# Forget sums and the split of the QKV weights moved into the QKV block; small loads of the modulation moved to ScalarE

## The reference, cut to what matters

```python
mod = (jax.nn.silu(c) @ w_ada + b_ada)[:, None, :]       # (1024) @ (1024, 6144)
sh1, sc1, g1, sh2, sc2, g2 = jnp.split(mod, 6, axis=-1)
h = rmsnorm(x, norm1_w) * (1 + sc1) + sh1
proj = h @ w_in                                          # z, x, B, C, dt | q, k, v | f
logf = jax.nn.log_sigmoid(f_raw + f_bias)                # per token and head, 8 heads
F_all = jnp.cumsum(jnp.concatenate([logf_prev, logf], axis=1), axis=1)
o = fox_attention(q, k_all, v_all, F_all[:, p0:], F_all, ...)   # scores + F_q - F_k
```

## Time and profile before

| what | us |
|---|---|
| median of 3 runs (lowest, highest) | 2694.07 (2690.8, 2696.57) |
| the profiled execution, its own time | 2693.54 |
| its span, first to last instruction | 2691.9 |
| busy: TensorE, VectorE, ScalarE, POOL | 2296.3, 1419.4, 944.6, 727.1 |
| mean granted clock of TensorE, of full | 0.921 |

### The profile page before, as it was taken

One profiled execution on the slowest core, in us unless ns is written; L12 is line 12 of the kernel. 1 busy time (PEld: TensorE's weight loads), 2 busy tenths in 40 slices (PEclk: granted clock), 3 DMA queues, 4 the chain that ended last, 5 costly groups with the idle time before them and its releaser, 6 DMA issues. The chain is left out here.

```text
span 2691.9 us, 35221 instructions
## 1 busy us (share of the span) xinstructions
PE 2296.3 (85%) x11464; PEld 1780.5 (66%) x11465; DVE 1419.4 (53%) x2897; ACT 944.6 (35%) x1628; POOL 727.1 (27%) x756
## 2 busy tenths in 40 slices
PE   3788989829999969999998599929999999999860
PEld 1687878726777845655564487718888888888650
DVE  1488878771001036666663567762445662435556
ACT  1354444321111114555554443321223441223533
POOL 0000101020000036777776002121323332222220
PEclk8899999959999969999999799959999999999985
DMA  6421211137774274544440644344657875557757
GB/s 194 162 73 64 78 59 70 48 119 249 256 260 171 104 170 113 111 92 86 86 85 18 226 150 143 120 165 109 186 173 242 270 246 153 161 157 220 226 188 265
DMA packets 190305, 408.39 MB, mean 152 GB/s; under 512 B 65274, under 2 KB 72728, under 8 KB 186784
## 3 DMA queue, kind: packets, MB, share of 16 engines
q1 hardware_dynamic: 161152, 304.51, 35.4%
q0 software_dynamic: 26672, 93.99, 12.8%
q10 hardware_dynamic: 2384, 8.65, 0.8%
HBM read 296.57 MB, written 110.53 MB: 151 GB/s over the span
## 5 line engine op out<-in xcount | busy, mean ns | idle before, releaser
L1391 POOL TENSOR_TENSOR c_acc<-c_acc,c_pr 128x512 f32<-128x512 f32 (+3 forms) x320 | 340.0, 1062 | 76.8 <-ACT c_pr L1513 34.8
L1513 ACT ACTIVATE c_pr<-c_ps,neg_f 128x512 f32<-128x512 f32 (+2 forms) x360 | 207.9, 595 | 162.7 <-PE c_ps L1457 154.4
L1543 DVE TENSOR_REDUCE c_mx<-c_pm 128x1 f32<-128x512 f32 (+3 forms) x304 | 178.8, 613 | 58.3 <-PE c_pm L1413 40.7
L1413 PE MATMUL c_pm<-c_km,c_q 66*128 66x512 f32 (+1 forms) x336 | 144.8, 447 | 22.6 <-DMA c_km<-f_k 16.5
L1176 DVE SCALAR_TENSOR_TENSOR b_lo<-b_pu,b_hi 128x512 fp32r<-128x512 f32 (+1 forms) x40 | 24.5, 612 | 258.7 <-ACT b_hi L1145 258.7
L258 PE MATMUL p_zx<-wa_hi,ah_hi 128*128 128x432 f32 x408 | 155.4, 381 | 3.6 <-DVE ah_lo L640 3.6
L258 PE MATMUL x_pg<-x_g_hi,x_x_hi 128*128 128x512 f32 x336 | 136.5, 406 | 24.8 <-DVE x_x_lo L2477 24.8
L607 POOL TENSOR_TENSOR yskip<-xs,params 128x512 f32<-128x512 f32 x17 | 21.6, 1268 | 497.6 <-ACT xs L545 497.6
L1466 PE MATMUL c_po<-c_pr,c_vv 128*64 128x512 f32 (+3 forms) x720 | 151.4, 522 | 0.0
L259 PE MATMUL p_zx<-wa_lo,ah_hi 128*128 128x432 f32 x408 | 150.2, 368 | 0.0
L260 PE MATMUL p_zx<-wa_hi,ah_lo 128*128 128x432 f32 x408 | 148.9, 365 | 0.0
(11 more groups left out here) (395 smaller groups left out, 5640.0 us busy)
## 6 DMA issues: line engine op xcount, KB each, us to landing
x_raw_g<-in_w_gate_dram SPq DMA_DIRECT2D x32, 1024.0 KB, 8.0
x_raw_u<-in_w_up_dram SPq DMA_DIRECT2D x32, 1024.0 KB, 8.6
x_raw_d<-in_w_down_dram SPq DMA_DIRECT2D x32, 1024.0 KB, 7.9
b_wa<-in_w_ada_dram POOLq DMA_DIRECT2D x16, 1024.0 KB, 7.6
c_k<-k_hi SPq DMA_DIRECT2D x14, 672.0 KB, 13.7
h_hi<-ah_hi SPq DMA_DIRECT2D x17, 512.0 KB, 2.6
h_lo<-ah_lo SPq DMA_DIRECT2D x17, 512.0 KB, 3.5
d_mix<-mix SPq DMA_DIRECT2D x17, 512.0 KB
```

The lines of the kernel that those rows point to most:

```text
L1391: pool.tensor_tensor(acc[:, ci % 2, cols], acc[:, ci % 2, cols], pr[:, i % RING, cols], ALU.add).then_inc(acc_done, 1)
L1413: last = pe.matmul(p_m[x % 2][:, 0:w * P], q2[0:KR, s, u["tile"] * P:(u["tile"] + 1) * P], km[:, s, kc], start=True, stop=not masked)
L1513: act.activation(pr[:, n % RING, cols], p_s[n % NPS][:, cols], ACT.Exp, bias=c.neg_f[:, it["h"], it["key"]:it["key"] + 1]).then_inc(exp_do ...
L1543: dve.tensor_reduce(mx[:, u % 2, pc["slot"]:pc["slot"] + 1], src, AX.X, ALU.max).then_inc(mx_done, 1)
```

## The change

In `modulation` the 11 small loads are issued by ScalarE at the head of its list. SP issues three slices of w_ada at once, into three places with a semaphore for each slice, and the fourth after the first chunk's products. `load_split_weights` has three places, so the load of slice k waits for the split of slice k - 3.

The stage `forget_sums` is gone. In the QKV block SP first issues two pairs of h, the last weight slice, the cached logs, and the third pair; ScalarE rounds the eight slices, VectorE splits all eight, and unit 0's products wait for each slice's split in turn. The sums become acts: after unit 0 the cached logs are transposed and the prompt's sum is taken, after units 1 and 2 the sum over the cached and the new tokens, after unit 3 the transposes of the 21 tiles. The negated halves of a sum lie in the memory of `b_wa`; each sum waits for the store of the one before, POOL's first load of w_ada waits for all three stores, and the first "first" act waits for `neg_out`. The modulation's acts start after unit 4 instead of unit 0.

```diff
-        wa = sb("wa", [P, 2, KD, CH])
+        wa = sb("wa", [P, 3, KD, CH])
-        small_loaded, params_loaded, wada_loaded = sem("small_loaded"), sem("params_loaded"), [sem("wada0"), sem("wada1")]
+        small_loaded, params_loaded, wada_loaded = sem("small_loaded"), sem("params_loaded"), [sem(f"wada{n}") for n in range(NFIRST)]
...
-            sp.dma_start(crow[0:8, :], row(a["c_prompt"][0])).then_inc(small_loaded, 16)
-            sp.dma_start(crow[8:16, :], row(a["c_sample"][0])).then_inc(small_loaded, 16)
-            for n in range(2):
-                sp.dma_start(wa[:, n], wsrc[:, :, n * CH:(n + 1) * CH]).then_inc(wada_loaded[n], 16)
-            for at, src in ((V_BADA, a["b_ada"][0]), (V_BADA + 48, a["b_ada_f"]), (V_N1, a["norm1_w"][0]),
-                            (V_N2, a["norm2_w"][0]), (V_NF, a["final_norm_w"]), (V_SSDW, a["ssd_norm_w"][0]),
-                            (V_ATTW, a["attn_norm_w"][0]), (V_CB, a["conv_b"][0])):
-                n = src.shape[0] // P
-                sp.dma_start(vrow[at:at + n, :], row(src)).then_inc(small_loaded, 16)
-            sp.dma_start(vrow[V_CW:V_CB, :], a["conv_w"][0].rearrange("i (j p) -> (i j) p", p=P)).then_inc(small_loaded, 16)
-            for n in range(2, NFIRST):
-                sp.wait_ge(mod_done, n - 1)
-                sp.dma_start(wa[:, n % 2], wsrc[:, :, n * CH:(n + 1) * CH]).then_inc(wada_loaded[n % 2], 16)
+            for n in range(NFIRST):
+                if n >= 3:
+                    sp.wait_ge(mod_done, n - 2)
+                sp.dma_start(wa[:, n % 3], wsrc[:, :, n * CH:(n + 1) * CH]).then_inc(wada_loaded[n], 16)
             load(sp)
...
         def _(act):
+            act.dma_start(crow[0:8, :], row(a["c_prompt"][0])).then_inc(small_loaded, 16)
+            act.dma_start(crow[8:16, :], row(a["c_sample"][0])).then_inc(small_loaded, 16)
+            for at, src in ((V_BADA, a["b_ada"][0]), (V_BADA + 48, a["b_ada_f"]), (V_N1, a["norm1_w"][0]),
+                            (V_N2, a["norm2_w"][0]), (V_NF, a["final_norm_w"]), (V_SSDW, a["ssd_norm_w"][0]),
+                            (V_ATTW, a["attn_norm_w"][0]), (V_CB, a["conv_b"][0])):
+                n = src.shape[0] // P
+                act.dma_start(vrow[at:at + n, :], row(src)).then_inc(small_loaded, 16)
+            act.dma_start(vrow[V_CW:V_CB, :], a["conv_w"][0].rearrange("i (j p) -> (i j) p", p=P)).then_inc(small_loaded, 16)
             act.wait_ge(small_loaded, 16 * 11)
...
-                pe.wait_ge(wada_loaded[n % 2], 16 * (n // 2 + 1))
+                pe.wait_ge(wada_loaded[n], 16)
...
-                mod_products(pe, ps[n % 2], c, wa[:, n % 2], range(KD), 0).then_inc(mod_done, 1)
+                mod_products(pe, ps[n % 2], c, wa[:, n % 3], range(KD), 0).then_inc(mod_done, 1)
...
-    stage = ctx.enter_context(nc.sbuf_tensor(f"{tag}_stage", [P, 2, width], F32))
-    loaded = [sem(f"stage_loaded{s}") for s in range(2)]
+    RING = 3
+    stage = ctx.enter_context(nc.sbuf_tensor(f"{tag}_stage", [P, RING, width], F32))
...
 
     def load(sp):
         for k in range(KD):
-            if k >= 2:
-                sp.wait_ge(split, k - 1)
+            if k >= RING:
+                sp.wait_ge(split, k - RING + 1)
             for lo, hi, src in chunks[k]:
-                sp.dma_start(stage[:, k % 2, lo:hi], src).then_inc(loaded[k % 2], 16)
+                sp.dma_start(stage[:, k % RING, lo:hi], src).then_inc(loaded[k % RING], 16)
 
     def round_hi(act):
         for k in range(KD):
-            act.wait_ge(loaded[k % 2], 16 * n_dma * (k // 2 + 1))
-            act.activation(w_hi[:, k, :], stage[:, k % 2, :], ACT.Copy).then_inc(rounded, 1)
+            act.wait_ge(loaded[k % RING], 16 * n_dma * (k // RING + 1))
+            act.activation(w_hi[:, k, :], stage[:, k % RING, :], ACT.Copy).then_inc(rounded, 1)
 
     def take_lo(dve):
         for k in range(KD):
             dve.wait_ge(rounded, k + 1)
-            dve.tensor_tensor(w_lo[:, k, :], stage[:, k % 2, :], w_hi[:, k, :].bitcast(F32), ALU.subtract).then_inc(split, 1)
+            dve.tensor_tensor(w_lo[:, k, :], stage[:, k % RING, :], w_hi[:, k, :].bitcast(F32), ALU.subtract).then_inc(split, 1)
 
     return load, round_hi, take_lo, split
...
-def forget_sums(nc, c, a, weights):
...
-    arrived = {(0, 0): 0, (0, 1): 0, (1, 2): 0, (1, 0): 1, (2, 1): 1, (2, 2): 1, (3, 0): 2, (3, 1): 2, (4, 2): 2}
-
+    arrived = {(0, 0): 1, (0, 1): 1, (1, 2): 1, (1, 0): 2, (2, 1): 2, (2, 2): 2, (3, 0): 3, (3, 1): 3, (4, 2): 3}
+    sums = [(0, SEQ), (TP, TK), (SEQ, TP)]
+
+    early_acts = {0: [("cache_f", 0), ("sum", 0)], 1: [("sum", 1)], 2: [("sum", 2)], 3: [("turn_f", 0)]}
...
                 yield "unit", u
-                if todo:
+                if u in early_acts:
+                    yield from early_acts[u]
+                elif todo:
                     yield todo.pop(0)
...
+        cl, F = sb("cl", [P, PAST // P, H]), c.scratch[0:H, :]
...
+        flat = lambda half: wa[0:H, half].rearrange("p k n -> p (k n)")
+        f_ones, f_hi, f_lo = flat(0), flat(1).bitcast(F32R), flat(0).bitcast(F32R)
...
+            weights.load_h(sp, c, 0, 0, h_loaded[0])
+            weights.load_h(sp, c, 1, 2, h_loaded[1])
+            for k in range(EARLY, KD):
+                weights.load(sp, k, w_loaded)
+            for t in range(PAST // P):
+                sp.dma_start(cl[:, t, :], a["cache_logf"][0, 0, t * P:(t + 1) * P, :]).then_inc(cl_loaded, 16)
+            weights.load_h(sp, c, 2, 6, h_loaded[2])
...
+                elif what == "sum":
+                    lo_, hi_ = sums[n]
+                    sp.wait_ge(f_split, n + 1)
+                    sp.dma_start(c.f_k[:, 0, lo_:hi_], f_hi[:, 0:hi_ - lo_].bitcast(F32)).then_inc(f_stored, 16)
+                    sp.dma_start(c.f_k[:, 1, lo_:hi_], f_lo[:, 0:hi_ - lo_].bitcast(F32)).then_inc(f_stored, 16)
...
+            sp.wait_ge(f_stored, 32 * len(sums))
...
         @block.gpsimd
         def _(pool):
+            pool.wait_ge(f_stored, 32 * len(sums))
...
-                    if arrived[n, pair] and (n, pair) not in seen:
+                    if (n, pair) not in seen:
...
                 for k in range(KD):
+                    if u == 0:
+                        pe.wait_ge(w_split, k + 1)
                     last = product3(pe, out, w_hi[:, k, cols], weights.lo(k)[:, cols], pick(h_hi, k), pick(h_lo, k), k == 0, k == KD - 1)
...
-                    if half == 0 and n > 4:
-                        pe.wait_ge(mod_biased, n - 4)
+                    if half == 0:
+                        if n > 4:
+                            pe.wait_ge(mod_biased, n - 4)
+                        else:
+                            pe.wait_ge(neg_out, 1)
...
+                elif what == "cache_f":
+                    pe.wait_ge(cl_loaded, 16 * (PAST // P))
+                    for t in range(PAST // P):
+                        last = pe.transpose(p_mod[0:H, t * P:(t + 1) * P], cl[:, t, :], c.ident[:])
+                    last.then_inc(cl_turned, 1)
+                elif what == "turn_f":
+                    pe.wait_ge(summed, len(sums))
+                    for t in range(NT_K):
+                        last = pe.transpose(p_mod[:, t * H:(t + 1) * H], F[:, t * P:(t + 1) * P], c.ident[0:H, 0:H])
+                    last.then_inc(f_turned, 1)
...
+                    elif un["j"] == 4:
+                        act.wait_ge(f_turned, 1)
+                        act.wait_ge(f_split, len(sums))
...
+            for k in range(KD):
+                if k >= EARLY:
+                    act.wait_ge(w_loaded, 16 * (k - EARLY + 1))
+                act.activation(w_hi[:, k, :], weights.raw(k), ACT.Copy).then_inc(w_rounded, 1)
...
+            dve.memset(f_ones, 1.0)
+            dve.memset(both[0:H, :], 1.0).then_inc(ones_set, 1)
+            for k in range(KD):
+                dve.wait_ge(w_rounded, k + 1)
+                dve.tensor_tensor(weights.lo(k), weights.raw(k), w_hi[:, k, :].bitcast(F32), ALU.subtract).then_inc(w_split, 1)
+            dve.wait_ge(ones_set, 1)
             for what, n in program():
-                if what == "unit":
+                if what == "cache_f":
+                    dve.wait_ge(cl_turned, 1)
+                elif what == "sum":
+                    lo_, hi_ = sums[n]
+                    w = hi_ - lo_
+                    src = p_mod[0:H, 0:PAST] if lo_ == TP else F[:, lo_:hi_]
+                    init = 0.0 if lo_ in (0, TP) else F[:, TK - 1:TK] if lo_ == SEQ else F[:, lo_ - 1:lo_]
+                    ones = f_ones if n == 0 else both[0:H, 0:w]
+                    dve.tensor_tensor_scan(F[:, lo_:hi_], ones, src, init, ALU.mult, ALU.add).then_inc(summed, 1)
+                    dve.wait_ge(summed, n + 1)
+                    if n >= 1:
+                        dve.wait_ge(f_stored, 32 * n)
+                    dve.tensor_scalar(f_hi[:, 0:w], F[:, lo_:hi_], -1.0, None, ALU.mult).then_inc(f_rounded, 1)
+                    dve.wait_ge(f_rounded, n + 1)
```

(85 more changed lines are left out.)

## The result

| | before | after |
|---|---|---|
| median (lowest to highest), us | 2694.83 (2690.8 to 2696.57) | 2656.02 (2652.83 to 2658.54) |
| the profiled execution, and its span | 2693.54, 2691.9 | 2658.54, 2656.9 |
| mean granted clock of TensorE | 0.921 | 0.926 |

The account below looks back on a forecast made before the run. Two stretches leaving TensorE idle, the modulation's start and the forget-sum stage, were taken as the bound. Modulation 16.0 us (7.8 + 8.2) plus QKV 15.4 (21.5 - 3.4 - 1.9 - 0.8) gave 31.4: 2693.5 to 2662 us, range 2654 to 2678.

Parts of the forecast that it names:

- The first product of the modulation: Modulation at the start: first product at 16 us instead of 24.8, with the first w_ada slice the later input.
- rival A: Modulation: rows do not pass the w_ada burst; stage gives 3.4 us instead of 16.0, total 2675 us; chance 0.14.
- The last scaling: End of the modulation's chunks: at 41.1 us, 7.8 us earlier, with 1 us allowed for lateness.
- Three places in the ring: Split of the SSD weights: eight slices end 16.8 us after the last scaling instead of 25.0, 8.2 us less.
- QKV's first unit: Start of the QKV block: unit 0 starts at 581.7 and ends at 589.1 instead of 610.6, 21.5 us sooner.
- What QKV has to carry: QKV: added costs of 3.4 us for transposes, 1.9 for the wait on POOL's load, 0.8 for a colder start.
- The moved transposes: QKV on TensorE: four of cached logs, 1.0 us, and 21 of the sums, 2.4 us, together +3.4 us.
- The wait on POOL's load: QKV: TensorE waits 6.8 us for POOL's w_ada load and 0.7 more over next units; +1.9 against before.
- colder start: QKV: 0.8 us added for TensorE's clock after the longer idle gap.
- Rival B: QKV: VectorE's sums keep long prices, 8.4 us more; QKV gives 7 us, total 2670.5 us; chance 0.12.
- Rival C: QKV: granted clock falls to 0.50 after the added wait and stays; slower, 2702 to 2788 us; chance 0.03.
- Rival D: Whole kernel: no change, rival A and Rival B together with last weight slice 5 us late; 2688 us; chance 0.04.

Follow-up runs that it names:

- the run with the later acts: Changed kernel with the modulation's acts of QKV starting four units later (after unit 8); 2646.83 us, ratio 0.9834 to the kernel before.

## Why the prediction was right, point by point

- **The first product of the modulation** (16 forecast, 17.54 measured): the loads by ScalarE pass the burst, so rival A falls. Which wait ends last was wrong: the rows, not the first slice of w_ada. What held them for 3.3 of their 15.95 us is POOL's loads of parameters: without these they landed that much sooner, and the first product still did not wait for w_ada.
- **The last scaling** (41.1; 41.9). The sum came out, but in part by luck: the first product came 1.5 us later than forecast, the 1 us allowed for a late slice was not needed, and the term of 6.0 us a chunk was taken as a constant, and it is a mean of two prices. A chunk takes 6.25 us, or 3.72 when TensorE is at its higher pace, and which of them comes when differs from one execution to the next. For this reason the stage gave 14.5 us in this profile and would have given 19.3 by the one whose next stage starts at 55.49 (its first split starts at 36.85); the profiled execution is the slowest of the four, and the medians' 38.8 against the profiles' 35.0 fits that.
- **Three places in the ring** (16.8 us; 17.5, and 17.8 alone): right, and the cycle through the slot was what bound it, since six places bring 11.4.
- **QKV's first unit** (first product 12.5 us into the block, end 19.9; 12.6 and 20.4): right; its start hangs on h, shown by the late slice put first.
- **What QKV has to carry** (+6.1; +1.5 from unit 0's end to attention, 347.85 before and 349.3 after): this is the step that was mis-sized. The moved transposes were put at 1.0 and 2.4 us, prices from a stage at a granted clock of 0.50. At 1.00 they last 0.60 and 1.46 us and hold up the next products by 0.35 (574.71 to unit 1's first product at 575.06) and 1.4: 1.7 instead of 3.4. The wait on POOL's load came to 7.1 as forecast (7.5); all of TensorE's idle time in this part grew by 1.2 us, from 11.2 to 12.4. The "colder start" of +0.8 shows in unit 0, which took 7.8 us instead of 7.2, but from there on the clock has the other sign. A stretch at 0.50 does follow the new wait, but the kernel before had such stretches too: 0.85 and 0.81 from 610 to 620 us, and these behind its own wait of 3.3 us for w_ada (windows of TensorE before):

```profile
640.00:645.00 5.00, 2.69 (x12) 0.58 1.04 400
645.00:650.00 5.00, 4.55 (x20) 0.73 1.12 340
```

TensorE's busy time, multiplied by the share of the clock that was not granted and summed over windows of 5 us, is 3.7 us before and 2.8 after. By this estimate the clock gives back 0.9, and 1.7 + 1.2 - 0.9 = 2.0 is near the 1.5 measured.

- **Rival B** did not happen, since the scans took 1.20 and 0.46 us, and its mechanism is real: with POOL busy the block takes 8.7 us more. That this is near the 8.4 it was given is chance, since 5.4 of these were for the scans of 512 and 128, which did not grow in that run.
- **Rival C** did not happen: behind the new wait the granted clock was 0.50 from 600 to 605 us, 0.92 in the next 5 and 1.00 after that. **Rival D** falls with A and B.

## What to carry to other kernels

Take the price of a TensorE instruction from a stretch at the clock level that the place it moves to will have; the transposes moved out of the idle stage lasted 0.6 of what they had. When many loads feed one wait, look at all queues: small loads of another engine can take much of the DMA engines' time (here 0.03 MB of them brought the rate from 381 down to 220 GB/s over 5 us), and moving them moves the cost. A wait that only comes from asking too early, as TensorE's for w_ada here, is cured by asking later, and here that was worth more than any further change to the loads at the start.

## What the runs showed of the hardware

TensorE's pace in the modulation is not what its granted-clock row says. The row of the changed kernel reads 1.00 where 16 products took 3.64 us, and so does the row of the run with the later acts where they took 1.92 (windows of TensorE, busy, granted clock, DMA, GB/s):

```profile
22.00:27.00 5.00, 5.00 (x24) 1.00 1.05 386
```

```profile
27.00:32.00 5.00, 3.36 (x31) 1.00 1.06 397
```

The ratio of 1.9 is that of the products of QKV's first unit (0.43 us apart at a granted clock of 0.50, 0.23 at 1.00), so the two prices look like the two levels, 1.2 and 2.4 GHz. The Trainium skill ("TensorE: Matmul & The Clock Gate", "Seeing it yourself") warns that the clock events of a trace can be unreliable; these rows bear that out from the start, where the row reads 1.00 before TensorE has run, to the row's first fall (in the changed kernel behind the modulation, 0.56 from 42 to 47 us). Before every rise TensorE had been busy, and the first products behind waits of 2.4 to 5.5 us were slow each time; why the rise came after one chunk in some executions and after three or more in others is open.
